# Token-half norm ahead of the joint attention, jobs moved out of a six-step down product, and an earlier vector activation

## The chip, the cores and the metric

The kernel runs on one core of one Trainium2 chip. The metric is the device time of one execution in microseconds (us); lower is better. Five engines work on their own instruction streams and meet at semaphores: TensorE (PE, matmuls), VectorE (DVE), ScalarE (ACT), GpSimd (POOL) and SyncE (SP, which here only starts the weight loads).

## The reference, cut to what matters

512 tokens of width 1024 pass through two blocks, all in float32. The first block has two layers; each is a mixer and a gated feed-forward. It ends in an RMS norm. The second block is modulated by a vector `c` and takes 256 context tokens with it: a joint attention, an MLP, a convolution mixer, an MLP.

```python
def first_block(x, ...):
    for layer in range(2):
        h = h + mixer(rmsnorm(h, mix_norm[layer]))
        h = h + swiglu(rmsnorm(h, ffn_norm[layer]), gate_up[layer], down[layer])
    return rmsnorm(h, final_norm)          # norm 4 of the kernel

def second_block(x, c, ctx, c_ctx, ...):
    mod = silu(c) @ ada_w[l] + ada_b[l]    # six vectors for each of 2 layers
    h = x * (1 + sc1) + sh1                # goes into the joint attention
    hc = ctx * (1 + csc1) + csh1
    x = layer_norm(ALPHA * x + g1 * attention(h, hc), ln_g, ln_b)
    x = layer_norm(ALPHA * x + g2 * mlp(x * (1 + sc2) + sh2), ln_g, ln_b)
    ...
```

## The kernel before, in words

Activations lie feature by token: `x` is [128, 8, 512], eight tiles of 128 features by 512 tokens. Every weight matrix is cut into units of 128 output features by up to 1024 inputs. A float32 product is made of three matmuls per step of 128 inputs: each weight tile is split into `w_hi` (ScalarE, a copy with rounding, L657) and `w_lo` (VectorE, the rest, L1275), each activation tile into `h_hi`/`h_lo` or `g_hi`/`g_lo`. A unit is thus 8 steps of 3 matmuls of 512 columns (`unit`, L2171), into PSUM bank 0 or 1.

Units go in pairs, `s` = 0 and 1, with two weight slots. `PLAN` is the list of stages and their units. On every engine `pairs(name, body, first, count)` loops over the pairs of a stage: ScalarE and VectorE first split the next unit's weights (`split_next`), then do the body, which takes the finished bank away. Engines keep program order, so a split that stands behind a body waits for it. SyncE loads a slot's next weights as soon as its last `w_lo` is done (L450).

The gated feed-forward runs in groups of 8, 8 and 6 hidden tiles; so `ffn0_down2` and `ffn1_down2` are products of six steps, 18 matmuls a unit, four pairs each. A last down product also prepares the norm behind it: its body adds the residual (L1346), squares the tile (L721, or L732 with `h_hi` made at L730), and GpSimd adds the squares up (L476). In `ffn0_down2` VectorE makes `h_lo` too (L1354).

**Jobs.** The 112 columns of modulation vectors are dot products of 1024 elements on VectorE: one load of 512 KB issued by ScalarE (`load_ada`, L677), one reduction (L1298) and one small add (L1301), `take_ada`. `ADA_PAIRS` says which stages carry a job per pair. `ffn0_down2` carries four, `mlp1_up0` none. The jobs read `c_row`, the silu of `c` and `c_ctx`. Ahead of the first job the stage `out0` activates it (`silu_of_rows`, L683), between the first and second eviction.

**Norm 4** stands between `ffn1_down2` and `attn_in`. It runs over whole tokens once the last unit is done: VectorE makes the small modulation columns (L1803 to L1816), closes the sum (L1333), TensorE sums over partitions (L2196), ScalarE takes the root (L773), VectorE inverts and spreads it on a diagonal (L1342), TensorE spreads it over partitions (L2206). Then, tile by tile, VectorE multiplies (L1823), ScalarE modulates and rounds (L1042, L1044), GpSimd makes `h_lo` (L512), and TensorE may start. After that ScalarE rescales `x` (L1046) and rounds the context (L1133), VectorE modulates the context (L1827) and makes its low part (L1831). The weights of the second unit of `attn_in` are split after all of it.

**Norms 5 to 8** run in token halves. `close_halves` does the last pair of the product in halves of 256 tokens (L2219), so that the first half's sums (L2229), root, diagonal and spreading (L2243) run beside the second half's matmuls. Four weight slots hold the two units of this pair and the first two or three of the next stage, split beforehand. `open_halves` starts the next stage on the first half by chunks of two tiles while the second is normalised. Norms 5 to 8 are layer norms: they also sum and centre (`xc`, L1982, L1991, L2024) and take a variance (L2002 to L2005). The half-wise changes of stage are `out2` to `mlp0_up0` (norm 5), `mlp0_down3` to `conv_in` (norm 6), `out3` to `mlp1_up0` (norm 7) and the end (norm 8).

```python
            def split_next(i, s):
                if s == 0:
                    split_hi(i, 1)
                elif not isinstance(i, int) or i < LAST_PAIR:
                    split_hi(i + 1, 0)
```

Of the kernel before, what the change touches and what calls it, by code (L numbers as in the profile page):

```python
# [66 lines left out]
ADA_STAGES = ["out0", "out1", "conv_in"] + [n for n, _ in PLAN if n[:3] == "ffn" or n[:4] == "mlp0"]  # L67
ADA_FIRST = {"out1": 1, "mlp0_up0": 2, "conv_in": 1}
ADA_PAIRS = {n: {"ffn1_down2": 2, "mlp0_down3": 2}.get(n, PAIRS[n] - ADA_FIRST.get(n, 0)) for n, _ in PLAN
# [96 lines left out]
def program(nc, dram, out):  # L166
    with ExitStack() as ctx:
# [293 lines left out]
        def _(pool):  # L461
# [21 lines left out]
            def centred_sums(r, tiles=range(KT)):  # L483

                both = ((N["xc"], N["s1"], xc_done, 6 * (r - 5), xc_half),
                        (N["sq"], N["s2"], sq_done, 5 * KT + 6 * (r - 5), sq_half))
                for k in tiles:
                    if 0 < k < KT - 2:
                        for src, acc, done, base, _ in both:
                            pool.wait_ge(done, base + k + 1)  # L490
                            landed(pool.tensor_tensor(acc[:], src[:, 0, :] if k == 1 else acc[:], src[:, k, :], ALU.add))  # L491
                    if k == KT - 2:
                        for half in range(2):
                            cols = half_cols(half)
                            for src, acc, _, _, done in both:
                                pool.wait_ge(done, halves_before(r, half, 2) + 1)
# [3 lines left out]
            def low_halves(r):  # L500

                for half in range(2):
                    for c in range(4):
                        part = (slice(None), slice(2 * c, 2 * c + 2), half_cols(half))
                        pool.wait_ge(y_hi, 5 * KT + halves_before(r, half, 4) + c + 1)
# [3 lines left out]
            def low(r, src):  # L509
                for k in range(KT):  # L510
                    pool.wait_ge(y_hi, KT * r + k + 1)
                    pool.tensor_tensor(h_lo[:, k, :], src[:, k, :], h_hi[:, k, :].bitcast(F32), ALU.subtract)\  # L512
                        .then_inc(h_ready, 1)
# [102 lines left out]
            sums(4)  # L616
            low(4, N["sq"])
# [22 lines left out]
        def _(act):  # L640
# [249 lines left out]
            p0 = PAIR0["out0"]  # L890
            load_ada("out0", p0, 0)
            first_residual(p0, 0, 0)
            split_next(p0, 1)
            silu_of_rows(c_row[:], 1)
            table_of_sqrt()
            first_residual(p0, 1, 1)
            pairs("out0", first_residual, 1)

            def ffn(layer, groups, after=None):
                for g, w in enumerate(groups):  # L900
# [16 lines left out]
                    else:  # L917
# [1946 lines left out]
```

## Time and profile before

| what | value |
|---|---|
| median of 3 runs | 2796.3 us (2791.69 to 2799.14) |
| the profiled execution | 2797.24 us, its span 2795.4 us |
| TensorE busy | 2660.7 us, 95% of the span |
| VectorE, ScalarE, GpSimd busy | 1595.2, 1047.2 and 262.9 us |
| granted TensorE clock, mean | 0.974 |

The span is what the trace shows; the execution's own time is 1.8 us more. Times of rows are us from the span's start. Engines other than TensorE are idle for a good part of the time, so what matters is where TensorE stands still, what ended each stand, and where its clock was granted at half (1.2 instead of 2.4 GHz).

### The profile page before, as it was taken

To read this page: it belongs to the slowest core of one execution; us is meant where nothing else is said; L and a number is where in the kernel's file an instruction comes from. 1 tells how busy PE (TensorE), PEld (TensorE's weight loads), DVE (VectorE), ACT (ScalarE), POOL (GpSimd) and SP (SyncE) were. 2 spreads that over 40 slices of the span, in tenths; PEclk is the share of its full clock that TensorE was granted. 3 is DMA by queue.
4 is the path that set the end of the run, shared out by engine and by line. 5 is a ranking of instruction groups with operands and counts; after the bars stand their busy time and mean duration, and the time that the engine had idled before them with its cause. 6 is when DMAs were issued, how large, how long until landed. Compare 5 with 4: busy or idle time off the path is not lost.

```text
span 2795.4 us, 38078 instructions
## 1 busy us (share of the span) xinstructions
PE 2660.7 (95%) x13122; PEld 2191.5 (78%) x13122; DVE 1595.2 (57%) x2499; ACT 1047.2 (37%) x1653; POOL 262.9 (9%) x200
## 2 busy tenths in 40 slices
PE   7999999999999999999979798889999899899997
PEld 6886788887889988888758476678888787788886
DVE  6754665656667756565542684365555665644446
ACT  5234422223347742222331365453233432433323
POOL 2310100001131010000110200020000300300002
PEclk9999999999989999999989899999999999999999
DMA  3221344444310034444422000124444243222222
GB/s 134 68 83 60 119 145 147 145 143 143 120 38 2 2 113 147 140 149 143 143 76 75 16 1 1 38 76 144 150 144 142 83 141 123 69 99 96 98 98 76
DMA packets 77702, 274.34 MB, mean 98 GB/s; under 512 B 8352, under 2 KB 11680, under 8 KB 77088
## 3 DMA queue, kind: packets, MB, share of 16 engines
q1 hardware_dynamic: 58560, 205.55, 21.9%
q10 hardware_dynamic: 19040, 67.43, 7.1%
q8 instruction: 65, 1.06, 0.2%
q14 instruction: 37, 0.30, 0.0%
HBM read 270.84 MB, written 2.10 MB: 98 GB/s over the span
## 4 chain that ended last, share of the span: by engine, by line
PE 82%; DVE 8%; ACT 5%; issue 3%; DMA 1%; ACTq 0%; POOL 0%; DVEq 0%; SPq 0%
PE banks L2171 60%; PE banks L2312 5%; PE banks L2605 3%; PE banks L2710 2%; PE banks L2219 2%; DVE w_lo L1275 2%; PE banks L2695 2%; PE banks L2573 1%; ACT w_hi L657 1%; PE banks L2588 1%; PE banks L2346 1%; PE banks L2675 1%; PE banks L2520 1%; DVE attn_nm L1911 1%; PE banks L2602 1%
## 5 line engine op out<-in xcount | busy, mean ns | idle before, releaser
L2171 PE MATMUL banks<-h_hi,w_hi 128*128 128x512 f32 x1616 | 636.3, 394 | 15.1 <-DVE w_lo L1275 9.7
L2171 PE MATMUL banks<-h_lo,w_hi 128*128 128x512 f32 x1616 | 632.3, 391 | 0.0
L2171 PE MATMUL banks<-h_hi,w_lo 128*128 128x512 f32 x1616 | 631.6, 391 | 0.0
L657 ACT ACTIVATE w_hi<-w_raw 128x1024 fp32r<-128x1024 f32 x371 | 390.1, 1052 | 563.2 <-PE banks L2171 445.8
L1275 DVE TENSOR_TENSOR w_lo<-w_raw,w_hi 128x1024 fp32r<-128x1024 f32 x371 | 487.6, 1314 | 161.3 <-ACT w_hi L657 143.5
L2171 PE MATMUL banks<-g_hi,w_hi 128*128 128x512 f32 (+1 forms) x1120 | 436.2, 389 | 21.3 <-DVE w_lo L1275 17.6
L2171 PE MATMUL banks<-g_lo,w_hi 128*128 128x512 f32 (+1 forms) x1120 | 430.1, 384 | 0.0
L2171 PE MATMUL banks<-g_hi,w_lo 128*128 128x512 f32 (+1 forms) x1120 | 429.8, 384 | 0.0
L2171 PEld LDWEIGHTS banks<-h_hi,w_hi 128*128 128x128 f32 x1616 | 305.1, 189 | 87.3 <-DVE w_lo L1275 13.0
L2171 PEld LDWEIGHTS banks<-h_hi,w_lo 128*128 128x128 f32 x1616 | 305.4, 189 | 64.3
L2171 PEld LDWEIGHTS banks<-h_lo,w_hi 128*128 128x128 f32 x1616 | 305.4, 189 | 62.2 <-issue 0.7
L2171 PEld LDWEIGHTS banks<-g_hi,w_hi 128*128 128x128 f32 x1120 | 212.0, 189 | 75.2 <-DVE w_lo L1275 28.2
L2171 PEld LDWEIGHTS banks<-g_lo,w_hi 128*128 128x128 f32 x1120 | 212.5, 190 | 41.6 <-issue 1.5
L2171 PEld LDWEIGHTS banks<-g_hi,w_lo 128*128 128x128 f32 x1120 | 212.2, 189 | 41.9
L1298 DVE CUSTOM_DVE_ANT_0 ada_raw<-ada_raw,rows_c 128x1024 f32<-128x1024 f32 x112 | 137.5, 1228 | 0.0
L1949 DVE SCALAR_TENSOR_TENSOR x<-banks,mod,x 128x512 f32 (+1 forms) x72 | 54.0, 750 | 140.9 <-PE banks L2171 140.2
L2312 PE MATMUL banks<-h_hi,w_hi 128*128 128x512 f32 x256 | 103.5, 404 | 12.2 <-DVE w_lo L1275 11.8
L2087 DVE TENSOR_TENSOR ffn_hid<-ffn_act 128x512 f32<-128x512 f32 x64 | 44.2, 691 | 100.4 <-ACT ffn_act L1219 100.4
L2312 PE MATMUL banks<-h_hi,w_lo 128*128 128x512 f32 x256 | 100.7, 393 | 0.0
L2312 PE MATMUL banks<-h_lo,w_hi 128*128 128x512 f32 x256 | 100.5, 392 | 0.0
L491 POOL TENSOR_TENSOR norm_s<-norm_xc 128x512 f32<-128x512 f32 x4 | 5.2, 1296 | 978.2 <-DVE norm_xc L1954 978.2
L1219 ACT ACTIVATE ffn_act<-banks 128x512 f32<-128x512 f32 x64 | 38.3, 598 | 149.7 <-PE banks L2171 144.8
(396 smaller groups left out, 3417.7 us busy)
## 6 DMA issues: line engine op xcount, KB each, us to landing
w_raw<-weights SPq DMA_DIRECT2D x384, 512.0 KB, 3.2
ada_raw<-ada ACTq DMA_DIRECT2D x112, 512.0 KB, 3.2
x<-x SPq DMA_DIRECT2D x4, 512.0 KB, 7.0
out<-x SPq DMA_DIRECT2D x8, 256.0 KB, 2.2
mix_cum<-ret_tab ACTq DMA_DIRECT2D x1, 1024.0 KB, 4.8
rows_c<-c_rows ACTq DMA_DIRECT2D x1, 1024.0 KB, 5.9
nsa_w<-cmp_w ACTq DMA_DIRECT2D x1, 1024.0 KB, 5.5
nsa_cbias<-nsa_cbias ACTq DMA_DIRECT2D x1, 1024.0 KB, 8.5
```

The source lines that it names most:

```text
L657: act.activation(w_hi[s][:], w_raw[s][:], ACT.Copy).then_inc(w_hi_done, 1)
L1219: act.activation(F["act"][:, s, :], psum[s], ACT.Relu).then_inc(bank_free[s], 1)
L1275: dve.tensor_tensor(w_lo[s][:], w_raw[s][:], w_hi[s][:].bitcast(F32), ALU.subtract)\
L1298: dve.tensor_tensor_reduce(ada_raw[:], ada_raw[:], c_row[:, who, :], 1.0, 0.0, ALU.mult, ALU.add, ada_col[:]).then_inc(ada_done, 1)
L1949: dve.scalar_tensor_tensor(xm, row(psum[s]), mod[:, bass.ds(8 * part + m, 1), 0], xm, ALU.mult, ALU.add).then_inc(bank_free[s], 1)
L2087: dve.tensor_tensor(F["hid"][:, s, :], F["act"][:, s, :], F["act"][:, s, :], ALU.mult)\
L2171: mm = pe.matmul(bank, w[s][:, k, :], m[:, k, :], start=(n == 0 and a == 0), stop=(n == kts - 1 and a == 2))
L2219: mm = pe.matmul(bank[:, cols], w[slot][:, k, :], m[:, k, cols], start=(k == 0 and a == 0), stop=(k == KT - 1 and a == 2))
L2312: mm = pe.matmul(bank, w[s][:, k, :], m[:, k, :], start=(k == 0 and a == 0), stop=(k == KT - 1 and a == 2))
L2605: mm = pe.matmul(o, S["v"][:, b, t, g, cols], S3["pt"][:, i % 2, b, t * P:(t + 1) * P], start=False, stop=(half == 1 and b == 1 and t == qi))
L2695: mm = pe.matmul(o, values[:, k, :], B4["pt"][:, t % 2, k * P:(k + 1) * P], start=(k == 0), stop=(k == KEY_TILES - 1))
L2710: mm = pe.matmul(banks[:, 2 + 2 * b + a, 0:c1 - c0], q, keys[:, c0:c1], start=True, stop=True)
```

## The change

Four edits, of which the first is large:

- Norm 4 runs in token halves. `ffn1_down2` keeps two ordinary pairs and goes through `close_halves`, now also for six steps (`kts`; of the second half of unit 0 five steps stand ahead of the sums, one behind), and `attn_in` begins with `open_halves`. For norm 4 the centring, the variance, and the matmuls of `s1` are skipped; the normalised tile is `x` times the scale and the gain of `final` is folded into the columns that ScalarE applies. The small modulation columns, nine instructions instead of seven, are made ahead of `ffn1_down2`. The load of the context is issued ahead of the closing pair, that of the rope table three pairs into `attn_in`. `x` is rescaled over the first four pairs of `attn_in`. The context's eight modulations stand behind the last normalised chunk, its low part is made in the second pair.
- `ffn0_down2` carries one job instead of four, in its first pair; three jobs go to pairs 1 to 3 of `mlp1_up0`.
- In `out0` ScalarE activates `c_row` ahead of the first eviction, and loads the table of the root after the second instead of between them.
- In `out0` VectorE takes the first job ahead of the second eviction instead of behind it.

```diff
-ADA_PAIRS = {n: {"ffn1_down2": 2, "mlp0_down3": 2}.get(n, PAIRS[n] - ADA_FIRST.get(n, 0)) for n, _ in PLAN
+ADA_FIRST = {"out1": 1, "mlp0_up0": 2, "conv_in": 1, "mlp1_up0": 1}
+ADA_PAIRS = {n: {"ffn0_down2": 1, "ffn1_down2": 2, "mlp0_down3": 2}.get(n, PAIRS[n] - ADA_FIRST.get(n, 0)) for n, _ in PLAN
...
             def last_product(name, r, gain=None):
                 table_of_sqrt()
-                if r > 4:
+                if r >= 4:
                     pairs(name, squares(r), 0, PAIRS[name] - 2)
+                    if r == 4:
+                        load_ctx()
                     close_halves(name, r, squares(r))
...
             p0 = PAIR0["out0"]
+            silu_of_rows(c_row[:], 1)
             load_ada("out0", p0, 0)
             first_residual(p0, 0, 0)
             split_next(p0, 1)
-            silu_of_rows(c_row[:], 1)
+            first_residual(p0, 1, 1)
             table_of_sqrt()
-            first_residual(p0, 1, 1)
...
+            def load_ctx():
+                act.wait_ge(ada_done, ADA_BEFORE_ATT)
+                act.dma_start(B3["ctx"][:], ...).then_inc(ctx_in, 16)
...
+            last_product("ffn1_down2", 4)
+            def settle_first(i, s, m):
+                act.activation(x[:, bass.ds(m, 1), :], N["xc"][:, bass.ds(m, 1), :], ACT.Copy,
+                               scale=ln_cols[:, bass.ds(24 + m, 1)]).then_inc(x_new, 1)
...
-            pairs("attn_in", nothing, 0, 6)
+            pairs("attn_in", settle_first, 1, 3)
+            act.dma_start(B3["rope"][:], ...).then_inc(att_in, 16)
...
             first_residual(p0, 0, 0)
             split_next(p0, 1)
-            first_residual(p0, 1, 1)
             dve.wait_ge(c_silu, 1)
             take_ada("out0", p0, 0)
+            first_residual(p0, 1, 1)
...
+                    if r == 4:
+                        dve.tensor_tensor(N["xc"][:, two, cols], x[:, two, cols], both(stat_half(half)), ALU.mult)\
+                           .then_inc(y_done, 1)
+                        return
...
+            pairs("ffn1_down2", add_residual, 0, 2)
+            close_halves("ffn1_down2", None, 4, add_residual)
+            dve.wait_ge(ctx_in, 16)
...
-                half_steps(psum[6], 0, 1, hi, lo, range(6))
+                half_steps(psum[6], 0, 1, hi, lo, range(6 if kts == KT else 5), kts)
                 sum_half(r, 0)
```

**Place 1, VectorE behind the last eviction of `ffn1_down2`.** Before, with the context and the split for the second unit of `attn_in` at the end:

```order
L1333 TENSOR_TENSOR norm_s_68<-norm_s_68,norm_sq 128x512 [waits dve_step,sq_done,acc_done]
L1339 RECIPROCAL norm_r<-norm_r 128x4 [waits root_done]
L1342 TENSOR_TENSOR norm_diag<-tab,norm_r 128x512 [waits dve_step]
L1823 SCALAR_TENSOR_TENSOR norm_y<-x,vec,banks 128x512 [waits scale_done]
L1823 SCALAR_TENSOR_TENSOR norm_y<-x,vec,banks 128x512 x7
L1827 TENSOR_SCALAR attn_ctx<-attn_ctx,mod 128x256 [waits ctx_in]
L1827 TENSOR_SCALAR attn_ctx<-attn_ctx,mod 128x256 x7
L1831 TENSOR_TENSOR g_lo<-attn_ctx,g_hi 128x256 [waits c_hi] x8
```

After, from the eviction of unit 1's first half (`more_w_lo` are the slots of units split ahead):

```order
L1868 TENSOR_TENSOR x<-x,banks 128x256 [waits unit_half]
L1295 TENSOR_TENSOR more_w_lo_127<-w_raw_55,more_w_hi_126 128x1024 [waits w_hi_done,bank_free0]
L1868 TENSOR_TENSOR x<-x,banks 128x256 [waits unit_half]
L1901 TENSOR_TENSOR norm_s_68<-norm_s_68,norm_sq 128x256 [waits sq_half,acc_done,bank_free1]
L1877 TENSOR_TENSOR x<-x,banks 128x256 [waits unit_done]
L1919 RECIPROCAL norm_r<-norm_r 128x2 [waits root_done,x_half]
L1922 TENSOR_TENSOR norm_diag<-tab,norm_r 128x256 [waits dve_step]
L1295 TENSOR_TENSOR w_lo_58<-w_raw_54,w_hi_56 128x1024 [waits w_hi_done]
L1943 TENSOR_TENSOR norm_xc<-x,banks 128x2x256 [waits scale_done]
```

The splits of three units of `attn_in` now stand ahead of the first normalised chunk, and four chunks of each half take the place of eight whole tiles; the context follows them.

**Place 2, ScalarE at the start of `out0`.** Before:

```order
L677 DMA ada_raw<-ada 128x1024
L730 ACTIVATE h_hi<-x,vec 128x512 [waits bank_free0]
L732 ACTIVATE norm_sq<-x 128x512
L657 ACTIVATE w_hi_56<-w_raw_54 128x1024 [waits unit_done,w_loaded0]
L683 ACT_TABLE_LOAD
L683 ACTIVATE rows_c<-rows_c 128x2048 [waits row_in]
L712 ACT_TABLE_LOAD
L712 ACTIVATE aux<-tab 128x1
L730 ACTIVATE h_hi<-x,vec 128x512 [waits bank_free1]
```

After:

```order
L682 ACT_TABLE_LOAD
L682 ACTIVATE rows_c<-rows_c 128x2048 [waits row_in]
L676 DMA ada_raw<-ada 128x1024
L729 ACTIVATE h_hi<-x,vec 128x512 [waits bank_free0]
L731 ACTIVATE norm_sq<-x 128x512
L656 ACTIVATE w_hi_56<-w_raw_54 128x1024 [waits unit_done,w_loaded0]
L729 ACTIVATE h_hi<-x,vec 128x512 [waits bank_free1]
L731 ACTIVATE norm_sq<-x 128x512
L711 ACT_TABLE_LOAD
L711 ACTIVATE aux<-tab 128x1
```

The activation and its table load moved ahead of both evictions and ahead of the first job's load; the root's table load moved behind the second eviction.

## Rows read from the trace of the kernel before

**Rows 1.** The chain that ended last, shares of the span by engine (the page).

```profile
PE 82%; DVE 8%; ACT 5%; issue 3%; DMA 1%; ACTq 0%; POOL 0%; DVEq 0%; SPq 0%
```

**Rows 2.** Norms 4, 5, 6, 7: window, us, busy us by engine, PEclk, DMA share.

```profile
1390.46:1436.29 45.83, 29.59 (x96) 20.22 (x94) 27.85 (x44) 23.35 (x40) 12.85 (x10) 0.74 0.28 92
1824.81:1864.33 39.52, 32.78 (x218) 30.83 (x216) 26.48 (x47) 19.57 (x35) 17.31 (x14) 0.87 0.21 67
2197.75:2236.86 39.11, 32.82 (x218) 30.86 (x216) 25.98 (x48) 19.84 (x36) 17.22 (x14) 0.87 0.20 67
2392.93:2433.54 40.61, 32.16 (x217) 30.27 (x216) 26.00 (x47) 19.69 (x35) 17.17 (x14) 0.87 0.20 65
```

**Rows 3.** Timeline of TensorE at norm 4: start us, us, engine, line.

```profile
1390.46 0.39 PE L2171 MATMUL banks<-g_hi,w_hi 128*128 128x512 f32 x1
...
1411.42 0.77 PE L2171 MATMUL banks<-h_hi,w_hi 128*128 128x512 f32 x1 [3.85 <-POOL h_lo L512]
...
1428.37 0.79 PE L2171 MATMUL banks<-h_hi,w_hi 128*128 128x512 f32 x1 [6.49 <-DVE w_lo L1275]
...
1436.29 0.39 PE L2171 MATMUL banks<-h_hi,w_hi 128*128 128x512 f32 x1
...
1441.73 0.39 PE L2171 MATMUL banks<-h_hi,w_hi 128*128 128x512 f32 x1
```

**Rows 4.** Timeline of VectorE at norm 4.

```profile
1400.10 0.18 DVE L1815 TENSOR_SCALAR aux<-vec 128x32 f32<-128x32 f32 x1
...
1412.88 8.78 DVE L1827 TENSOR_SCALAR attn_ctx<-attn_ctx,mod 128x256 f32<-128x256 f32 x8
...
1427.09 1.22 DVE L1275 TENSOR_TENSOR w_lo<-w_raw,w_hi 128x1024 fp32r<-128x1024 f32 x1
```

**Rows 5.** Timeline of TensorE at norm 6, the changes of phase.

```profile
2208.61 0.56 PE L2219 MATMUL banks<-g_hi,w_hi 128*128 128x256 f32 x1
...
2213.59 0.59 PE L2243 MATMUL banks<-norm_diag,tab 128*128 128x256 f32 x2
...
2218.25 0.35 PE L2219 MATMUL banks<-h_hi,w_hi 128*128 128x256 f32 x1 [4.07 <-POOL h_lo L506]
...
2225.62 0.59 PE L2243 MATMUL banks<-norm_diag,tab 128*128 128x256 f32 x2
```

**Rows 6.** What paces the first half's sums at norm 6, ScalarE and VectorE.

```profile
2203.03 1.06 ACT L663 ACTIVATE more_w_hi<-w_raw 128x1024 fp32r<-128x1024 f32 x1 [0.55 <-DMA w_raw<-weights]
...
2206.42 0.60 DVE L1991 TENSOR_TENSOR norm_s<-norm_s,norm_xc 128x256 f32<-128x256 f32 x1
```

**Rows 7.** DMA issues at norm 4: KB each, us to landing.

```profile
attn_ctx<-ctx ACTq DMA_DIRECT2D x1, 1024.0 KB, 6.4
```

**Rows 8.** Timeline of VectorE in `ffn0_down2`.

```profile
671.62 1.63 DVE L1275 TENSOR_TENSOR w_lo<-w_raw,w_hi 128x1024 fp32r<-128x1024 f32 x1 [0.59 <-ACT w_hi L657]
...
676.33 1.65 DVE L1275 TENSOR_TENSOR w_lo<-w_raw,w_hi 128x1024 fp32r<-128x1024 f32 x1 [0.58 <-ACT w_hi L657]
677.90 1.21 DVE L1298 CUSTOM_DVE_ANT_0 ada_raw<-ada_raw,rows_c 128x1024 f32<-128x1024 f32 x1
...
682.71 1.63 DVE L1275 TENSOR_TENSOR w_lo<-w_raw,w_hi 128x1024 fp32r<-128x1024 f32 x1 [0.59 <-ACT w_hi L657]
```

**Rows 9.** Timelines of ScalarE, VectorE and TensorE at the start of `out0`.

```profile
286.64 0.72 ACT L730 ACTIVATE h_hi<-x,vec 128x512 fp32r<-128x512 f32 x1 [3.68 <-DVE x L1346]
...
288.85 1.28 ACT L683 ACT_TABLE_LOAD   x1
290.14 1.92 ACT L683 ACTIVATE rows_c<-rows_c 128x2048 f32<-128x2048 f32 x1
...
294.89 2.31 DVE L1298 CUSTOM_DVE_ANT_0 ada_raw<-ada_raw,rows_c 128x1024 f32<-128x1024 f32 x1
...
298.74 0.50 PE L2171 MATMUL banks<-g_hi,w_hi 128*128 128x512 f32 x1 [2.86 <-DVE w_lo L1275]
```

**Rows 10.** Timeline of VectorE in `mlp1_up0`.

```profile
2457.66 0.69 DVE L2087 TENSOR_TENSOR ffn_hid<-ffn_act 128x512 f32<-128x512 f32 x1 [1.07 <-ACT ffn_act L1219]
```

More of the change, by code:

```diff
@@ L504, in low_halves @@
                         part = (slice(None), slice(2 * c, 2 * c + 2), half_cols(half))
-                        pool.wait_ge(y_hi, 5 * KT + halves_before(r, half, 4) + c + 1)
+                        pool.wait_ge(y_hi, 4 * KT + halves_before(r, half, 4) + c + 1)
                         pool.tensor_tensor(h_lo[part], N["sq"][part], h_hi[part].bitcast(F32), ALU.subtract)\
                             .then_inc(h_ready, 1)
[L509 to L513, printed above, removed]
             def nsa_side():
@@ L615, in _ @@
             sums(3)
-            sums(4)
-            low(4, N["sq"])
+            centred_sums(4)
+            low_halves(4)
             pool.wait_ge(att_in, 16)
@@ L1155, in rope_steps @@
                                        ACT.Copy).then_inc(bk_copied, 1)
-            pairs("attn_in", nothing, 0, 6)
-            pairs("attn_in", nothing, 6, 2)
-            pairs("attn_in", nothing, 8, 1)
+            pairs("attn_in", settle_first, 1, 3)
+            act.dma_start(B3["rope"][:], dram["rope_tab"].rearrange("p (c t) -> p c t", c=2)).then_inc(att_in, 16)
+            pairs("attn_in", nothing, 4, 5)
             act.wait_ge(lam_sum, 1)
@@ L1828, in _, with ctx_low @@
                                   ALU.mult, ALU.add).then_inc(ctx_h, 1)
-            for k in range(KT):
+            def ctx_low(k):
                 dve.wait_ge(c_hi, k + 1)
@@ L1854, in take2 @@
                 return body
-            pairs("attn_in", take(lambda m: B2["aq"][:, bass.ds(m, 1), :], 0.125), 0, 2)
+            p0, take_aq = PAIR0["attn_in"], take(lambda m: B2["aq"][:, bass.ds(m, 1), :], 0.125)
+            take_aq(p0, 0, 0)
+            take_aq(p0, 1, 1)
+            for s in range(2):
+                split_next(p0 + 1, s)
+                for k in range(4 * s, 4 * s + 4):
+                    ctx_low(k)
+                take_aq(p0 + 1, s, 2 + s)
             pairs("attn_in", take2(lambda m: B2["ak"][:, bass.ds(m - 4, 1), :]), 2, 2)
@@ L2147, in _ @@
             pairs("conv_in", gated, 8, 4)
-            dve.wait_ge(ada_taken, ADA_JOBS)
+            dve.wait_ge(ada_taken, ADA_JOB0["mlp1_up0"])
             modulations((10,), (2,))
@@ L2207, in spread_scales, with half_steps @@
                     .then_inc(scale_done, 1)
-            def norm(r):
-                square_means(r)
-                spread_scales(r)
-            def half_steps(bank, slot, half, hi, lo, steps):
+            def half_steps(bank, slot, half, hi, lo, steps, kts=KT):
                 cols = half_cols(half)
```

399 lines of the change are left out of this document (211 added, 188 removed).

## Prediction

> **What bounds the kernel now.** I read the chain of waits first: TensorE holds 82% of it [rows 1], so only an edit that lets TensorE start sooner, or at the full clock, changes the time. Work taken off or put on another engine counts where TensorE waits for that engine. Then I cut the trace at the changes of stage and compared the four places where a norm stands between two products [rows 2]. The last pair of the product and the first pair of the next stage take 45.83 us at norm 4, which runs over whole tokens, and 39.52, 39.11 and 40.61 us at norms 5 to 7, which run in halves, although theirs have eight steps in the closing pair and norm 4's has six. The reader should also see PEclk: 0.74 against 0.87. With only the two levels, 0.74 means that 52% of 45.83 us, 24 us, ran at 1.2 GHz; 0.87 means 10 us. Third, the timeline of TensorE at norm 4 [rows 3]: the closing pair starts at 1390.46, the first matmul of `attn_in` at 1411.42, its second unit only at 1428.37, the next pair at 1436.29. The wait of 6.49 us ahead of the second unit ends with a `w_lo` at 1427.09, which stood on VectorE behind the 8.78 us of the context [rows 4]. Last come the timelines of the engines in `ffn0_down2`, `out0` and `mlp1_up0` [rows 8 to 10].
>
> **Norm 4 in halves.** I build the new stretch from norm 6, whose chain is in the trace, in five phases.
>
> *a. Closing pair to the first half's sums.* At norm 6 it takes 2208.61 - 2197.75 = 10.86 us [rows 2, 5]. It does not follow the matmul count, since the fourth weight slot is split at 2203.03 on a weight load that it waited for [rows 6], and the squares stand behind it. So the six steps save nothing here. What norm 4 has no use for is the centring sum (0.60 us [rows 6]) and the centring and sum matmuls, which I put at 0.8 us, an estimate from the same row. I take 9.4 us.
>
> *b. Sums to spreading.* 2213.59 - 2208.61 = 4.98 us with 6 + 24 half-width matmuls [rows 5], 0.166 us each. Norm 4 has 3 + 18: 3.5 us. The root, the reciprocal and the diagonal are ready inside that, as at norm 6.
>
> *c. Spreading to the first opened matmul.* 2218.25 - 2213.59 = 4.66 us [rows 5]: one VectorE product, one chunk on ScalarE, one on GpSimd, all the same. 4.7 us.
>
> *d. To the second half's spreading.* 2225.62 - 2218.25 = 7.37 us [rows 5]. Centring and variance go; from the 0.6 us a step that they take I subtract two: 6.1 us, an estimate.
>
> *e. To the next pair.* 2236.86 - 2225.62 = 11.24 us [rows 2, 5], set by ScalarE's chunks, which do not change. 11.2 us.
>
> Sum: 9.4 + 3.5 + 4.7 + 6.1 + 11.2 = 34.9 us. The issue of the context's load stands on ScalarE's queue ahead of a split that is already late; I add 0.35 us. The stretch is then 35.2 us instead of 45.8: **10.6 us less**. Bounds: 39.11 us, norm 6 as it is [rows 2], and 32.5 us, if phase a shrinks with its matmuls too. The nine small modulation instructions in front of `ffn1_down2` stand where seven took from 1400.10 to 1401.5, 0.2 us each [rows 4]: 1.9 us, where VectorE otherwise waits for ScalarE's table load and split, so all but **0.3 us more** is covered. The cover is that wait; without it, 1.9.
>
> What is behind the halves: the context. Its load of 1024 KB lands 6.4 us after issue [rows 7], some 25 us before VectorE turns to it; it shares the queue's engines with one weight load, for which I allow nothing beyond the bounds. Its eight modulations (up to 8.78 us [rows 4], as long as GpSimd works beside them) end about when the first pair of `attn_in` does. The split that waits behind them is for the second unit of the next pair, due 5.44 us later (1441.73 - 1436.29 [rows 3]), and needs 2.3 us of ScalarE and VectorE. So 3 us of slack. The rescaling of `x` and the rope load lie beside full TensorE pairs: nothing.
>
> **Jobs out of `ffn0_down2`.** The loop is a ring: `w_lo`, eviction, `h_hi`, square, `w_hi`, `w_lo`. Each turn is one unit. Without a job it took 676.33 - 671.62 = 4.71 us, with one 682.71 - 676.33 = 6.38 us [rows 8], because the reduction and its add stand in front of the eviction. TensorE needs only 18 x 0.227 = 4.1 us (5.44 / 24 [rows 3]) and waits for `w_lo` in either turn. A job is thus worth 1.67 us. Three leave, from pairs 1, 2 and 3; the last one stands behind the last `w_lo` that TensorE waits for in this stage, and its eviction has a whole unit of `nsa_in` to be late in. So two count: **3.3 us less**, between 2.0 and 5.0.
>
> **Jobs into `mlp1_up0`.** VectorE idles 1.07 us ahead of such a turn's body [rows 10] and a job takes 1.67, so 0.6 us of it is not covered by that idle time; the rest of the turn has slack for most. **0.3 us more**, between 0 and 1.2.
>
> **`out0`.** ScalarE waits 3.68 us for the first eviction [rows 9]; the table load and the activation take 1.28 + 1.92 = 3.20 us and fit in. But the first job (2.31 us [rows 9]) now stands in front of the second eviction, and the root's table load (1.28 us and 0.2) in front of the split that TensorE waits 2.86 us for. Adding up, the eviction ends at 293.2, `h_hi` and the square at 294.6, the table at 296.1, `w_hi` and `w_lo` at 298.4, against 298.7 now: **0.3 us less**, between 0 and 1.4 (the latter if the first job takes what the others take, 1.21 [rows 8]). In the trace the activation starts at 290.14, when the table load of 1.28 us from 288.85 has just ended, and nothing stands between [rows 9]. The Trainium skill speaks against this place: "ScalarE: Activation LUTs", What ACT_TABLE_LOAD costs, puts a switch at 2.66 us, with 1.38 us of drain. By it the activation would need 4.6 us, 0.9 more than the wait holds, and the sum for `out0` would be a loss of 0.6 us. The rows show no such drain here, and the sum goes by them.
>
> **Sum.** -10.6 + 0.3 - 3.3 + 0.3 - 0.3 = -13.6 us against the profiled execution's own 2797.24 us (span 2795.4). That execution is 0.9 us above the median of 2796.3, within the spread of the three; I take 13.6 off the median: **2782.7 us**. A measurement of this kernel can tell about 0.3%, 8.4 us, from no change, so the line lies at 2787.9.
>
> **Rivals.**
>
> 1. *Norm 4's halves take as long as norm 6's.* All of a half-wise stretch is paced by the other engines; if the weight loads and ScalarE's chunks set it in every phase, nothing is saved on six steps. For it: norms 5 to 7 are within 1.5 us of each other [rows 2]. Against it: the centring is on the chain there. The stretch is 39.1 and the gain 6.7: 2796.3 - 9.7 = 2786.6 us. Chance 0.14.
>
> 2. *The context gives part of it back.* If GpSimd's work, the context's modulations and the splits behind them run on past the 3 us of slack, TensorE waits in the second pair of `attn_in` for a `w_lo`, the same stall as the one removed but shorter. With all 6.49 us of it [rows 3]: 2789.2 us. Chance 0.09.
>
> 3. *TensorE's clock stays at 1.2 GHz.* Six steps give TensorE less to do beside the norm's chain: in phase a it has 51 half-width matmuls in 9.4 us, and waits again in c. It fell to 1.2 GHz in every norm's stretch before [rows 2]. If it stayed there through the whole of the new one and the next pair, 84 full matmuls' worth and 48 more take 0.227 us more each: 30.0 us, less the 5.1 us that norm 6's 10 us at half clock already cost: +24.9. Then the kernel is slower: 2796.3 - 13.6 + 24.9 = 2807.6 us. It decides from 60 full matmuls at the lower level beyond norm 6's share (13.6 / 0.227). Against it: norms 5 to 7 returned to full clock with gaps as long, at a mean of 0.87. Chance 0.03.
>
> 4. *The jobs were covered in `ffn0_down2`.* If a turn without a job is filled by another wait, on a weight load or on TensorE, the 3.3 us are not gained. Alone this gives 2786.0 us, inside my case's range; together with rival 1 it gives 2789.9 us, and that pair has a chance of 0.03. Against it: the turn of 4.71 us without a job stands in the same loop [rows 8].
>
> **How the numbers follow.** My case, 0.71, spans 2778 to 2787. Faster by more than 0.3% takes it, rival 1 and a third of rival 2: 0.87. Within 0.3%: 0.10. Slower: 0.03. The range must leave out no more than 2 in 10: its lower end is all bounds taken well, 13.3 - 0.3 + 5.0 + 1.4 = 19.4 us, 2777; its upper end takes in rival 1 with the badly taken bounds of the small edits, 2789.
>
> **What would show it.** In the profile after: a closing and opening stretch of 35 us at norm 4, with PEclk near 0.87 and no TensorE wait above 5 us; no wait for `w_lo` in the second pair of `attn_in`; two turns in `ffn0_down2` at 4.7 instead of 6.4 us; a `w_lo` in `out0` within 1.5 us of its place; at most one short wait in `mlp1_up0`. I am wrong if the stretch is above 39 us, if the stall of 6.49 us comes back elsewhere, or if the clock stays low.

## The result, and the profile after

The changed kernel takes 2780.6 us, the median of 6 runs (2779.3 to 2784.5), against 2793.8 us (2791.2 to 2799.1) for the kernel before on the same chip: a ratio of 0.9946, with a 95% interval of 0.9936 to 0.9956, or 15.1 us less (12.3 to 17.9). The two medians themselves are 13.2 us apart; all comparisons below go by the ratios and their intervals. The prediction was 13.6 us less. A second set of runs of the change gave 0.9945 (0.9931 to 0.9958). The profiled execution took 2779.32 us (span 2777.5 us, mean granted clock 0.978); its span is 17.9 us shorter than that of the execution shown of before.

The chain of waits has the same bound as before [rows 1]:

```profile
PE 82%; DVE 8%; ACT 5%; issue 3%; DMA 1%; POOL 0%; ACTq 0%; DVEq 0%; SPq 0%
```

The windows of norm 4 and of norms 5 to 7 after the change, with the columns of [rows 2]; the first runs from the closing pair of `ffn1_down2` to the second pair of `attn_in`:

```profile
1383.97:1420.26 36.29, 27.54 (x182) 25.85 (x180) 24.09 (x35) 22.27 (x45) 13.91 (x11) 0.86 0.22 73
1808.50:1847.00 38.50, 31.50 (x218) 29.52 (x218) 26.51 (x47) 19.81 (x35) 17.19 (x14) 0.91 0.21 69
2179.80:2219.10 39.30, 32.89 (x218) 30.92 (x217) 25.85 (x48) 19.81 (x36) 17.22 (x14) 0.87 0.20 67
2375.10:2415.30 40.20, 32.43 (x218) 30.53 (x216) 25.89 (x47) 19.68 (x35) 17.12 (x14) 0.87 0.21 66
```

The stretch is 36.29 us instead of 45.83, with PEclk 0.86 instead of 0.74; norms 5 to 7 are what they were. TensorE's timeline there, at the changes of phase that the prediction uses (start, duration, in brackets the wait and what ended it):

```profile
1383.97 0.28 PE L2260 MATMUL banks<-g_hi,w_hi 128*128 128x256 f32 x1
...
1393.70 0.61 PE L2270 MATMUL banks<-tab,norm_s 128*128 128x1 f32 x4 [3.27 <-DVE norm_s L1901]
1394.17 0.36 PE L2260 MATMUL banks<-g_hi,w_hi 128*128 128x256 f32 x1
...
1398.08 0.79 PE L2285 MATMUL banks<-norm_diag,tab 128*128 128x256 f32 x2
...
1402.92 0.55 PE L2260 MATMUL banks<-h_hi,w_hi 128*128 128x256 f32 x1 [4.06 <-POOL h_lo L511]
...
1408.89 0.59 PE L2285 MATMUL banks<-norm_diag,tab 128*128 128x256 f32 x2
...
1420.26 0.47 PE L2217 MATMUL banks<-h_hi,w_hi 128*128 128x512 f32 x1 [0.17 <-DVE attn_aq L2018]
```

The wait of 6.49 us for `w_lo` [rows 3] is gone. What is left are two waits of 3 to 4 us, for the first half's sum and for its first `h_lo`, and the whole norm had both too (3.27 and 3.85 us in the profile of before). VectorE now meets the context behind the norm's last product:

```profile
1411.92 6.57 DVE L1999 TENSOR_SCALAR attn_ctx<-attn_ctx,mod 128x256 f32<-128x256 f32 x8
...
1419.42 1.40 DVE L2018 TENSOR_SCALAR attn_aq<-banks 128x512 f32<-128x512 f32 x2 [0.71 <-PE banks L2260]
1421.61 1.23 DVE L1289 TENSOR_TENSOR w_lo<-w_raw,w_hi 128x1024 fp32r<-128x1024 f32 x1 [0.80 <-ACT w_hi L656]
```

In `out0` the early silu, the first job in front of the second eviction, and the unit that waits for the split behind it, which answer to [rows 9]:

```profile
283.96 1.91 ACT L682 ACTIVATE rows_c<-rows_c 128x2048 f32<-128x2048 f32 x1
...
289.69 1.22 DVE L1312 CUSTOM_DVE_ANT_0 ada_raw<-ada_raw,rows_c 128x1024 f32<-128x1024 f32 x1
...
293.07 1.28 ACT L711 ACT_TABLE_LOAD   x1
...
295.54 1.23 DVE L1289 TENSOR_TENSOR w_lo<-w_raw,w_hi 128x1024 fp32r<-128x1024 f32 x1 [2.23 <-ACT w_hi L656]
...
296.82 0.50 PE L2217 MATMUL banks<-g_hi,w_hi 128*128 128x512 f32 x1 [1.25 <-DVE w_lo L1289]
```

And in `ffn0_down2` VectorE's splits [rows 8], from the stage's first turns to the last, now without a job between them (the last four turns; the job that stays is in the first pair):

```profile
677.09 1.67 DVE L1289 TENSOR_TENSOR w_lo<-w_raw,w_hi 128x1024 fp32r<-128x1024 f32 x1 [0.58 <-ACT w_hi L656]
...
681.84 1.74 DVE L1289 TENSOR_TENSOR w_lo<-w_raw,w_hi 128x1024 fp32r<-128x1024 f32 x1 [0.48 <-ACT w_hi L656]
...
686.64 1.65 DVE L1289 TENSOR_TENSOR w_lo<-w_raw,w_hi 128x1024 fp32r<-128x1024 f32 x1 [0.58 <-ACT w_hi L656]
...
691.38 1.75 DVE L1289 TENSOR_TENSOR w_lo<-w_raw,w_hi 128x1024 fp32r<-128x1024 f32 x1 [0.49 <-ACT w_hi L656]
```

Turns of 4.75, 4.80 and 4.74 us stand where 6.38, 4.69 and 6.36 stood. Cut at the same marks, the two profiled executions compare so:

| stretch | before, us | after, us | difference |
|---|---|---|---|
| first matmul to `out0` | 256.5 | 255.6 | -0.8 |
| `out0` (its first matmul to the next stage's) | 62.6 | 59.3 | -3.3 |
| `ffn0_down2`, likewise | 43.0 | 39.5 | -3.5 |
| the rest, up to norm 4's closing pair | 1028.4 | 1029.5 | +1.1 |
| norm 4's stretch | 45.8 | 36.3 | -9.5 |
| all behind it | 1359.2 | 1357.2 | -1.9 |
| span | 2795.4 | 2777.5 | -17.9 |

The first line holds clock. The sixth holds mostly clock, and the jobs in `mlp1_up0`. Of the fourth, 0.5 us stand ahead of the first matmul and 0.4 in the stages from `out1` to the closing pair, where the small modulations now are. TensorE is granted 1.2 GHz for short times, mostly in the same stages in every profile but not always for as long, and stages that no edit touches differ from one profile to the next: from the first matmul to `out0` it is 254.8 to 258.9 us, from `nsa_in` to `out1` 286.6 to 289.9. So the sizes of the terms have to come from several profiles.

### The profile page after: what moved, and what is told of

It reads as the page before. It is cut to its first block, busy times and chain, and to the rows that moved or that the text cites. A ratio compares the mean times of both kernels' runs of the same rounds, so it can differ in the third digit from the quotient of the medians.

```text
span 2777.5 us, 38210 instructions
## 1 busy us (share of the span) xinstructions
PE 2653.7 (96%) x13208; PEld 2191.8 (79%) x13208; DVE 1595.3 (57%) x2506; ACT 1050.6 (38%) x1664; POOL 263.2 (9%) x201
## 3 DMA queue, kind: packets, MB, share of 16 engines
q8 instruction: 66, 1.08, 0.2%
## 4 chain that ended last, share of the span: by engine, by line
PE 82%; DVE 8%; ACT 5%; issue 3%; DMA 1%; POOL 0%; ACTq 0%; DVEq 0%; SPq 0%
PE banks L2217 59%; PE banks L2354 5%; PE banks L2648 3%; PE banks L2260 2%; PE banks L2751 2%; DVE w_lo L1289 2%; PE banks L2736 2%; PE banks L2616 1%; ACT w_hi L656 1%; PE banks L2631 1%; PE banks L2388 1%; PE banks L2716 1%; DMA w_raw<-weights 1%; PE banks L2563 1%; DVE attn_nm L2092 1%
## 5 line engine op out<-in xcount | busy, mean ns | idle before, releaser
L2217 PE MATMUL banks<-h_hi,w_hi 128*128 128x512 f32 x1600 | 627.5, 392 | 3.9 <-DVE w_lo L1289 3.4
L2217 PE MATMUL banks<-h_lo,w_hi 128*128 128x512 f32 x1600 | 624.2, 390 | 0.0
L2217 PE MATMUL banks<-h_hi,w_lo 128*128 128x512 f32 x1600 | 623.9, 390 | 0.0
L2217 PE MATMUL banks<-g_hi,w_hi 128*128 128x512 f32 (+1 forms) x1108 | 429.3, 387 | 18.1 <-DVE w_lo L1289 14.6
L2217 PE MATMUL banks<-g_lo,w_hi 128*128 128x512 f32 (+1 forms) x1108 | 423.7, 382 | 0.0
L2217 PE MATMUL banks<-g_hi,w_lo 128*128 128x512 f32 (+1 forms) x1108 | 423.6, 382 | 0.0
L2354 PE MATMUL banks<-h_hi,w_hi 128*128 128x512 f32 x256 | 103.9, 406 | 12.5 <-DVE w_lo L1289 12.3
L2354 PE MATMUL banks<-h_hi,w_lo 128*128 128x512 f32 x256 | 101.0, 394 | 0.0
L2354 PE MATMUL banks<-h_lo,w_hi 128*128 128x512 f32 x256 | 100.9, 394 | 0.0
```

The costliest lines, as they stand in the source:

```text
L2217: mm = pe.matmul(bank, w[s][:, k, :], m[:, k, :], start=(n == 0 and a == 0), stop=(n == kts - 1 and a == 2))
L2354: mm = pe.matmul(bank, w[s][:, k, :], m[:, k, :], start=(k == 0 and a == 0), stop=(k == KT - 1 and a == 2))
```

## The experiments

Theory A, with which the experiments began: the gain is the sum of three separate terms, norm 4 (9.5 us in the profile), the jobs in `ffn0_down2` (3.3) and the order of `out0` (1.6, and perhaps as much again for the clock). The rivals: the clock or a single stall carries most of it. The ratios, each to the kernel before on the same chip:

| kernel | ratio | 95% interval |
|---|---|---|
| the change | 0.9946 | 0.9936 to 0.9956 |
| e1: norm 4 whole again | 0.9974 | 0.9964 to 0.9983 |
| e2: jobs back | 0.9954 | 0.9942 to 0.9966 |
| e3: `out0` back | 0.9955 | 0.9942 to 0.9968 |
| e4: root's table early | 0.9941 | 0.9929 to 0.9954 |
| e5: context doubled | 0.9952 | 0.9937 to 0.9967 |
| e6: whole norm, context behind a split | 0.9963 | 0.9949 to 0.9977 |
| e7: job behind the eviction | 0.9926 | 0.9912 to 0.9940 |
| e9: sums first | 0.9943 | 0.9929 to 0.9957 |
| e11: sums first, mended, and root early | 0.9903 | 0.9887 to 0.9918 |
| e12: the kernel before, again | 0.9998 | 0.9989 to 1.0007 |
| e13: the change, again | 0.9945 | 0.9931 to 0.9958 |

An interval is 3 to 4 us wide to either side, so single terms of 1 to 3 us are read from the profiles, and the ratios only say whether a sum of them holds.

**e1, norm 4 whole again.** The kernel before with the two small parts of the change alone:

```diff
-ADA_PAIRS = {n: {"ffn1_down2": 2, ...
+ADA_PAIRS = {n: {"ffn0_down2": 1, "ffn1_down2": 2, ...
...
+            silu_of_rows(c_row[:], 1)
             load_ada("out0", p0, 0)
...
             take_ada("out0", p0, 0)
+            first_residual(p0, 1, 1)
```

> The change with norm 4 put back to whole tokens (jobs and out0 as in the change). Theory A (the norm is the largest part, 9.5 us of the profile, and adds up with the rest): 2789.5 to 2791, some 3 to 4 us under the kernel before, and the closing and opening stretch back at 45 to 46 us with a w_lo wait of about 6.5 us ahead of the second unit of attn_in. Rival B (the small edits and the clock carry most of it): 2784 or less, 9 us or more under the kernel before.

It took 2788.7 us, 7.3 us under the kernel before (4.8 to 10.1) and 7.8 us over the change. Its norm's window:

```profile
1386.02:1430.35 44.33, 27.42 (x95) 18.36 (x94) 27.88 (x44) 23.36 (x40) 12.86 (x10) 0.81 0.28 95
```

The stall of 6.49 us is in it to the hundredth. Norm 4 is the largest part, but the small edits are worth more than the 3 to 4 us of theory A. In the profile they are 3.2 us in `out0` (59.4 against 62.6) and 3.5 us in `ffn0_down2`, 6.7 together.

**e2, the jobs back.**

```diff
-ADA_STAGES = [..., "conv_in", "mlp1_up0"] + ...
+ADA_STAGES = [..., "conv_in"] + ...
...
-ADA_PAIRS = {n: {"ffn0_down2": 1, "ffn1_down2": 2, ...
+ADA_PAIRS = {n: {"ffn1_down2": 2, ...
...
```

> The change with the three jobs put back into ffn0_down2 and taken out of mlp1_up0. Theory A (the ring of VectorE and ScalarE sets ffn0_down2, so a job costs its own 1.67 us there): three turns of 6.4 us again, from the first w_lo of the stage to the one of the next stage 32.8 us instead of 29.5, and 3.0 to 3.5 us more than the change, 2783.5 to 2784. Rival B (the stage's gain came from an interval of 3.4 us at half clock that happened not to fall there): 1.7 us or less more, with the half-clock interval deciding and not the turns. Rival C (mlp1_up0 pays for what ffn0_down2 gains): no difference, and waits for w_lo in mlp1_up0 of the change that this kernel does not have.

It took 2784.3 us, 2.2 us more than the change by the ratios. `ffn0_down2` takes 43.0 us again, as before, and 39.5 in the change. There is no interval at 1.2 GHz in this stage, while in the profile of the kernel before there was one (at 686); the turn beside it took 6.36 us there and the one at full clock 6.38. So rival B falls by the profile: the ring sets the turn, and TensorE's clock is hidden in it. Rival C has a part: from the end of the wait in the second pair of `mlp1_up0` to the first matmul of `mlp1_down0` it is 27.41 us here and 27.94 in the change, 0.5 us for the three jobs. This run also had the shortest norm 4, 33.78 us. TensorE stayed at the full clock for nearly all of it, and VectorE's split of the fourth slot took 1.22 us where it took 1.76 in the change:

```profile
1389.04:1422.82 33.78, 25.18 (x182) 23.38 (x180) 23.44 (x35) 22.32 (x44) 14.60 (x11) 0.95 0.23 78
```

**e3, the order of `out0` back.**

```diff
-            silu_of_rows(c_row[:], 1)
             load_ada("out0", p0, 0)
...
             split_next(p0, 1)
-            first_residual(p0, 1, 1)
+            silu_of_rows(c_row[:], 1)
             table_of_sqrt()
+            first_residual(p0, 1, 1)
```

(and on VectorE the job behind the eviction, as before.)

> The change with the order of out0 as before: silu and both table loads between the evictions, the first job behind the second eviction. Theory A (the job takes 2.31 us there because GpSimd's sum of squares runs beside it, and 1.22 us in front of the eviction): the first job at 2.3 us again, the w_lo of the second split 1.6 us later, TensorE waiting about 2.9 us. Whether an interval at 1.2 GHz follows, as it did in the kernel before, decides between 1.6 and 3.3 us more than the change. Rival B (the sum of the prediction): 0.3 us more. Rival C (a switch of tables costs more than its load, so the early silu loses): this kernel is faster than the change.

It took 2783.7 us, 2.5 us more than the change by the ratios. Its timeline has the long job and TensorE's wait of before:

```profile
296.15 2.31 DVE L1312 CUSTOM_DVE_ANT_0 ada_raw<-ada_raw,rows_c 128x1024 f32<-128x1024 f32 x1
...
298.72 1.22 DVE L1289 TENSOR_TENSOR w_lo<-w_raw,w_hi 128x1024 fp32r<-128x1024 f32 x1
...
300.00 0.50 PE L2217 MATMUL banks<-g_hi,w_hi 128*128 128x512 f32 x1 [2.82 <-DVE w_lo L1289]
```

`out0` takes 60.9 us, 1.6 more than in the change, and the interval at 1.2 GHz did not follow. Rivals B and C fall by the profile; the ratios alone, with intervals that overlap, would not tell.

**e4, the root's table early.** Measured from the change, on ScalarE:

```diff
             split_next(p0, 1)
-            first_residual(p0, 1, 1)
             table_of_sqrt()
+            first_residual(p0, 1, 1)
```

> The change with the root's table load in front of the second first_residual of out0 on ScalarE, where ScalarE is idle for 3.28 us, instead of behind it. Theory A (the load of 1.28 us and the 0.2 us stand on the path to the split that TensorE waits for): w_lo 1.4 us earlier, TensorE's wait of 1.25 us gone, 1.0 to 1.3 us less than the change, about 2779.5. Rival B (the wait has another cause, the weight load or VectorE): no difference.

The wait of 1.25 us is gone, `out0` takes 58.1 us, 1.2 less. The total, 2780.1 us, is 1.4 us less by the ratios, too little to tell in the time alone. The table load's place was on the path.

**e5, the context doubled.**

```diff
-                dve.tensor_scalar(B3["ctx"][:, k, :], ..., modcol(1, k, 1), modcol(0, k, 1), ALU.mult, ALU.add)
+                landed(dve.tensor_scalar(B3["ctx"][:, k, :], ..., modcol(1, k, 1), None, ALU.mult))
+            for k in range(KT):
+                dve.tensor_scalar(B3["ctx"][:, k, :], ..., modcol(0, k, 1), None, ALU.add)
```

> The change with each of the context's eight modulations in two instructions (multiply, then add), some 6 us more on VectorE in front of the splits of the second pair of attn_in. Theory A (about 2.9 us of slack: w_lo is ready at 1422.84 and needed at 1425.70 in the profile of the change): one wait of TensorE of 3 to 4 us for that w_lo, and as much more time. Rival B (the context was already on the path, so all of it costs): 6 us or more. Rival C (it is far from the path): nothing, no wait.

It took 2782.8 us, a ratio that tells no difference from the change. VectorE's timeline behind the norm:

```profile
1412.05 6.71 DVE L1999 TENSOR_SCALAR attn_ctx<-attn_ctx,mod 128x256 f32<-128x256 f32 x8
1418.79 2.19 DVE L2001 TENSOR_SCALAR attn_ctx<-attn_ctx,mod 128x256 f32<-128x256 f32 x8
...
1421.12 1.27 DVE L2020 TENSOR_SCALAR attn_aq<-banks 128x512 f32<-128x512 f32 x2
1422.78 1.23 DVE L1289 TENSOR_TENSOR w_lo<-w_raw,w_hi 128x1024 fp32r<-128x1024 f32 x1 [0.39 <-ACT w_hi L656]
```

and TensorE's first matmul of the second pair:

```profile
1421.94 0.47 PE L2219 MATMUL banks<-h_hi,w_hi 128*128 128x512 f32 x1 [1.61 <-DVE attn_aq L2020]
```

The edit was smaller than meant: the second eight instructions take 2.19 us, 0.27 each, where the first take 0.84. All three expectations miss the place. TensorE waits 1.61 us, and not for a `w_lo` but for the eviction of the first unit, `attn_aq`, which stands between the context and the split; the `w_lo` at 1422.78 is in time. In the change that wait is 0.17 us, so 2.2 us of work cost 1.44: the slack was about 0.7 us and not 2.9, which fits the 0.71 us that VectorE idled ahead of that eviction in the change.

**e6, a whole norm with the context behind a split.** From e1, on both engines:

```diff
+            split_next(PAIR0["attn_in"], 0)
             dve.wait_ge(ctx_in, 16)
             for k in range(KT):
                 dve.tensor_scalar(B3["ctx"][:, k, :], ...
```

> Norm 4 over whole tokens as in e1_norm_whole, with one thing changed: the first split of attn_in stands ahead of the context on ScalarE and VectorE instead of behind it. It tells how much of the gain is the context's stall of 6.49 us and how much the halves. Theory A (the stall is removed whole, and the halves bring only the rest): the wait ahead of the second unit gone, the stretch 38 to 39.5 us against 44.4 in e1_norm_whole, and 5 to 6 us less than that kernel, about 2783. Rival B (the halves are what counts; the stall comes back in front of the next pair): the stretch above 42 us, at most 2 us less.

The window from the closing pair to the second pair of `attn_in`, and VectorE's timeline in it:

```profile
1384.64:1423.31 38.67, 27.17 (x95) 18.02 (x93) 22.03 (x45) 24.33 (x41) 12.87 (x10) 0.82 0.28 95
```

```profile
1414.07 1.46 DVE L1279 TENSOR_TENSOR w_lo<-w_raw,w_hi 128x1024 fp32r<-128x1024 f32 x1 [7.53 <-ACT w_hi L657]
1415.45 2.67 DVE L1831 TENSOR_SCALAR attn_ctx<-attn_ctx,mod 128x256 f32<-128x256 f32 x8
```

On ScalarE the split stands ahead of the rescaling of `x` and the rounding of the context as well. The stretch falls from 44.33 to 38.67 us by this order alone, 5.7 us, as theory A says; a wait of 1.99 us for the other split appears ahead of the next pair. The halves leave 33.8 to 37.9 us in six profiles, so they add between 0.8 us (against the three with the same clock, 0.82, which take 37.8 to 37.9) and 4.9, in the mean 2.0 against this one profile. The total, 2788.0 us, tells it the other way round: 3 us under e1, where theory A put 5 to 6, and 5 over the change by the ratios. All these intervals overlap. Both parts are there, but which of them is the larger is not shown.

**e7, the job behind the eviction.** The change, with VectorE's order of before:

```diff
-            dve.wait_ge(c_silu, 1)
-            take_ada("out0", p0, 0)
             first_residual(p0, 1, 1)
+            dve.wait_ge(c_silu, 1)
+            take_ada("out0", p0, 0)
```

> The change with only the first job of out0 put back behind the second eviction (silu stays early, the root's table load late). Theory A (the job took 2.31 us in the kernel before because GpSimd's sum of squares ran beside it): it takes 2.2 to 2.4 us here too, from 291.9, and the split waits for it until 294.2 and ends 295.4, against 296.8 in the change: about 1.2 us less time than the change. Rival B (the job was long because it followed the late silu or was the first one): it takes 1.2 us here; then w_hi at 294.1 sets the split. Rival C (the job's place in front of the eviction is what gained 1.6 us in the change): 1 us or more slower than the change.

All engines of e7 in that stretch:

```profile
294.95 1.34 POOL L480 TENSOR_TENSOR norm_s<-norm_sq 128x512 f32<-128x512 f32 x1 [111.47 <-ACT norm_sq L731]
295.06 2.31 DVE L1312 CUSTOM_DVE_ANT_0 ada_raw<-ada_raw,rows_c 128x1024 f32<-128x1024 f32 x1
```

The job takes 2.31 us as theory A says, though silu was early: GpSimd's addition began 0.11 us before it and ended at 296.29, and the job ended 1.08 us later. The second unit no longer waits: `out0` takes 58.2 us, 1.1 less than in the change. Rival B falls by the duration, rival C by the sign. The place in front of the eviction is not what gained. e3 has the same order on VectorE and differs from e7 on ScalarE alone, and its `out0` takes 2.8 us more: the early activation gained, and the job's new place gave part of that back. The total, 2776.6 us, is 5.6 us under the change by the ratios, more than the 1.1 us that `out0` explains; where the rest comes from is not shown, and the profiled execution, with a span of 2779.9 us, does not have it.

**e9, the sums first.** From the change, in the closing pairs of norms 4 to 7; VectorE and then ScalarE:

```diff
                 take(0, 0)
-                if more:
-                    split_lo_to(3, i + 1, 1)
                 take(0, 1)
                 close(0)
+                if more:
+                    split_lo_to(3, i + 1, 1)
...
-                if more:
-                    split_hi_to(0, i + 2, 0, 2 * i + 1)
                 root_half(0)
...
                     chunk(0, 0)
+                    split_hi_to(0, i + 2, 0, 2 * i + 1)
```

> The change with the closing pairs of norms 4 to 7 in another order: on VectorE the last quarter of the residual and the first half's sums stand ahead of the fourth slot's split, and the first chunk ahead of the split after it; on ScalarE the root and the first chunk ahead of that split. Theory A (phase a of a half-wise norm is set by a weight split that is needed only 10 us later, not by the sums' own chain): the wait of 3.27 us ahead of the sums' matmuls falls to about 1.6 us at norm 4 and by 1.2 us at norms 5 to 7, 4 to 6 us less than the change, 2775 to 2777. Rival B (the later release of the raw weights delays the next loads, and the time is given back as waits for w_lo): no gain, or a loss up to 4 us.

It took 2783.4 us, 0.8 us less than the change by the ratios, which is no gain that can be told, and norm 4's stretch is 37.86 us. The wait for the first half's sum falls from 3.27 to 1.33 us, as theory A says, and later the time is given back, as rival B says, but for another reason than a late load:

```profile
1403.35 1.45 DVE L1294 TENSOR_TENSOR w_lo<-w_raw,w_hi 128x1024 fp32r<-128x1024 f32 x1 [2.83 <-ACT w_hi L662]
```

ScalarE took this split up at 1402.28, behind the first chunk, with 4.02 us of idle time ahead of that chunk; the second half's sum stands behind it on VectorE.

**e11, mended.** The split ahead of the chunk on ScalarE, and e4's edit with it:

```diff
                 square(1, 0)
                 if more:
+                    split_hi_to(0, i + 2, 0, 2 * i + 1)
                     act.wait_ge(aux_done, max(1, r - 4))
                     chunk(0, 0)
-                    split_hi_to(0, i + 2, 0, 2 * i + 1)
```

> e9_sums_first with its one fault mended (ScalarE's split of the slot after next stands ahead of the first chunk, where ScalarE waits 4.02 us, instead of behind it), and the early root load of e4_root_early. Theory A (e9 gained 1.9 us in phase a and lost it because VectorE waited 2.83 us for that split in front of the second half's sums): no wait above 1 us for that split, the sums' wait at norm 4 stays at 1.3 to 1.6 us, 1 to 2 us less at each of norms 4 to 7 and 1.2 us at out0, 2773 to 2776. Rival B (the halves are paced by VectorE's and GpSimd's work whatever the order): only the 1.2 us of out0, 2779.

It took 2769.3 us, a ratio of 0.9903: 27 us under the kernel before and 11.8 under the change (e13, on the same chip). Norm 4's window, and TensorE at the first half's sum:

```profile
1382.36:1416.90 34.54, 27.50 (x181) 25.88 (x180) 22.98 (x35) 22.60 (x45) 13.69 (x11) 0.85 0.22 77
```

```profile
1390.45 0.61 PE L2269 MATMUL banks<-tab,norm_s 128*128 128x1 f32 x4 [1.32 <-DVE norm_s L1900]
```

The wait is 1.32 us and the stretch 34.54, 1.9 less than in e13 at nearly the same clock. This is the version that beats both. The spans of e11 and e13 differ by 8.2 us, of which `out0` is 1.2, norm 4 1.9, norm 5 0.7, norm 6 2.2 and norm 7 1.6. Norm 6's 36.8 us and norm 5's 37.5 lie below those of all other profiles (38.6 to 41.1 and 38.1 to 40.1). Norm 7's 38.5 does not, for e3 has the same without the edit, and norm 4's 34.54 is above the 33.78 of e2. The excess of 11.8 over 8.2 is not explained.

**e12 and e13, both kernels again.**

> The kernel before, once more, for its clock. Theory A (the interval of 3.4 us at 1.2 GHz at the second pair of out0 belongs to its wait of 2.86 us): it is there again and out0 takes 62.6 us from its first matmul to the next stage's. Rival B (where such an interval falls is not fixed by the program): it is absent, and out0 takes 60.9 us, as in e3_out0_back. The norm 4 stretch is 44 to 46 us.

> The change once more, beside e11_split_between on the same chip, and for the spread of norm 4's stretch: 34 to 38 us by the four profiles so far of kernels that share it (33.9 to 38.1), out0 59.3 us, ffn0_down2 39.5 us, and 13 to 16 us less than the kernel before.

e12 took 2796.0 us and e13 2781.1, 14.9 us apart. In e12 an interval of 3.4 us at 1.2 GHz stands at the second pair of `out0` once more, which takes 62.0 us; norm 4's stretch is 44.48. In e13 the stretch is 36.44, `out0` 59.3 and `ffn0_down2` 39.5. TensorE's interval at 1.2 GHz in `out0` was there in two of the three profiles with TensorE's wait of 2.8 us (before and e12, not e3) and in none of the ten with a shorter wait. That ties it to the wait without fixing it; it is worth 1.0 to 1.6 us there (62.0 and 62.6 against 60.9).

## Why the prediction was right, term by term

The sum was 13.6 us, and the measured gain is 15.1 us (12.3 to 17.9), 14.9 between e12 and e13. The terms, each by all profiles that bear on it:

| term | predicted | measured |
|---|---|---|
| norm 4's stretch | -10.6 | -8.2: whole 45.83, 44.48, 44.33; halves 36.29, 36.44, 33.78, 37.93, 37.94, 37.78 |
| small modulations ahead of `ffn1_down2` | +0.3 | +0.4: TensorE's wait behind them, in the first pair of `ffn1_down2`, is 1.62 instead of 1.20 us |
| jobs out of `ffn0_down2` | -3.3 | -3.5 |
| jobs into `mlp1_up0` | +0.3 | +0.5 |
| `out0` | -0.3 | -1.6, and -2.7 to -3.3 with the clock |
| sum | -13.6 | -12.4, and -13.5 to -14.1 with the clock |

That the total came so near is in part luck. Norm 4 was put 2.4 us too high and `out0` 1.3 us too low (2.4 to 3.0 with the clock), and the two misses cancel.

**Norm 4.** The prediction's phase a ends with the first product matmul behind the first half's sums, at 1394.17 in the profile of the change. Cut at its marks, that profile has 10.20, 3.91, 4.84, 5.97 and 11.37 us, where the prediction put 9.4, 3.5, 4.7, 6.1 and 11.2. The largest miss is phase a, 0.8 us too short, and it is not clock: TensorE's matmuls stand at the full rate, 0.12 us apart, until 1395.0. VectorE's split of the fourth slot, behind which the residual and the first half's sums stand, met GpSimd's addition:

```profile
1390.51 0.72 POOL L502 TENSOR_TENSOR norm_s<-norm_s,norm_sq 128x256 f32<-128x256 f32 x1
1390.55 1.76 DVE L1295 TENSOR_TENSOR more_w_lo<-w_raw,more_w_hi 128x1024 fp32r<-128x1024 f32 x1 [0.98 <-ACT more_w_hi L662]
```

In e2 the split takes 1.22 us and phase a 9.33. e9 and e11, where it stands behind the sums, have 8.48 and 8.56. Phase b is 0.4 us too short: it was scaled by its matmuls from norm 6, but 14 of its 21 half-width ones ran at 1.2 GHz, 0.213 us apart instead of 0.119. So the term that was mis-sized is norm 4's, on both sides. Its new stretch was put at 35.2 us from one norm of one execution, and six profiles have 36.7 in the mean, 33.8 to 37.9. It was set against one whole norm of 45.8 us that was 1.4 us longer than two others. Rival 1 did not happen, for all six lie below norm 6's 39.1 us. Nor did rival 3: the clock was 0.82 to 0.95 in the stretch.

**What in norm 4 gained.** The prediction named the stall of 6.49 us but costed only the halves. In the profiles of e1 and e6, 5.7 us of the stretch go with the split's place ahead of the context, without any halves, and the halves take 0.8 to 4.9 us more. The whole times give the halves the larger part, 5 us against 3. The forecast of the stretch held within 1.5 us in the mean, but its reason, the overlap of half norms with products, is only one of two, and the sizes of the two are not settled.

**The context behind it.** "So 3 us of slack" was wrong. It was counted to the `w_lo`, and the eviction of the first unit, which stands on VectorE between the two, was left out. e5 measures about 0.7 us. The load landed 5.3 us after its issue at 1376.7 (6.4 [rows 7]), and VectorE did not wait for it. The modulations took 6.57 us instead of the 8.78 allowed, a difference larger than the real slack, and that kept rival 2 away.

**The jobs.** The ring's turn with and without a job, and which two of three count, came out as put. Rival 4 is refuted by e2's profile.

**`out0`.** The term came out 1.3 us too small, and the step that failed is the first job's price. The prediction carried its 2.31 us from [rows 9] to the new place; it is 1.22 there. The bound of 1.4 us, with 1.21 for the job, was the right value, and the reason for it was in the trace: the sum of squares on GpSimd. That the early silu fits into ScalarE's wait held: the table load and the silu were over at 285.87, and `h_hi` then waited 0.46 us for the eviction. The loss of 0.6 us by the figure of the Trainium skill, "ScalarE: Activation LUTs", What ACT_TABLE_LOAD costs, did not come.

**The rest of `mlp1_up0`.** One short wait of 0.18 us was added, and turns a little longer; 0.5 us, inside the bounds.

## What to carry to other kernels

Before costing a new structure, find what stands in the queue between the long wait and its releaser: here the stretch of a whole norm fell by 5.7 us when one weight split was put ahead of eight small instructions. Count slack to the first instruction in the queue that anyone waits for, evictions included. A duration taken from a row holds only with the same company: look what GpSimd does beside a VectorE instruction before its price is moved. And where the clock changes for short times, one profile does not carry a term of 2 us: here the same stretch took 33.8 to 37.9 us in six.

## What the runs showed of the hardware

**VectorE blocked by GpSimd.** The job took 1.22 us alone and 2.31 us when it began 0.1 us behind a GpSimd addition of 1.34 us (e7, e3, e12 and the kernel before); it ended 1.08 us after the addition in e7, so at most 0.14 us of its 1.22 were done beside it. It goes the other way too. In e2 the split of the fourth slot began 0.33 us ahead of GpSimd's addition and kept its 1.22 us; the addition took 1.47 us instead of the 0.72 shown above. The context's modulations took 0.27 us each with GpSimd idle (e5's second eight) and 0.84 beside `h_lo` (e5's first eight), 0.33 in e6 with GpSimd idle, 0.82 beside `h_lo` in the change and 1.10 in the kernel before. The job and the split show no slowing in proportion but waiting for the other's end. The Trainium skill, "SBUF — State Buffer", section "SBUF: two separate sides", says so: GpSimd and a VectorE instruction with two SBUF inputs or in a two-port mode share a port pair, whichever starts first holds it for its whole instruction, and the other blocks fully. By that rule the job in e7 would end one duration after the addition, at 297.5, an estimate; the trace has 297.37.

**A table switch costs its load.** In all thirteen profiles the activation of `c_row` in `out0` begins 0.01 us after the load of 1.28 us has ended, as in e7:

```profile
285.89 1.28 ACT L682 ACT_TABLE_LOAD   x1
287.18 1.91 ACT L682 ACTIVATE rows_c<-rows_c 128x2048 f32<-128x2048 f32 x1
```

The drain of 1.38 us that the Trainium skill, "ScalarE: Activation LUTs", What ACT_TABLE_LOAD costs, adds to each switch is in no row of these kernels: in the change ScalarE's work ahead of this load ended 0.02 us before it, and wherever a later activation did begin late, it waited for another engine's result. The measurement decides here.
